# Where a Trainium2 network's tables begin: split weights 32 and 64 bytes from the split activations

## What is computed

```python
for i in range(2):                       # sparse attention, then an RWKV-7 mixer
    x = x + (dsa_mixer, rwkv7_mixer)[i](rms_norm(x, mixer_norm[i]), ...)
    x = x + sqrelu_mlp(rms_norm(x, mlp_norm[i]), w_up, w_down)   # relu(h @ w_up)**2 @ w_down
# then a short-convolution mixer and a dilated-attention mixer, each
h, gate = adaln_pre_norm(x, c, g, w_mod, b_mod)
x = x + gate * mixer(h, w_in, w_out)
return rms_norm(x)
```

## The kernel before

| table | remainder by 128 |
|---|---|
| `raw`, `w_hi`, `w_lo`, `X`, `const` (all slots) | 0 |
| `act_hi`, `act_lo`, set 0 and set 1 (all pieces) | 64 |
| `ff_hi`, `ff_lo` (both slots, all pieces) | 64 |
| `w_idx_hi`, `w_idx_lo`, piece kt (288 bytes each) | 64 + 32 kt |

## Time and profile before

### The profile page before, as it was taken

The page is one execution under the profiler, slowest core; times in us unless marked ns, Lnnn a source line. Parts: engine busy times, 40 slices in busy tenths (PEclk is TensorE's granted clock), DMA queues, the critical chain, the costliest instruction groups (busy, mean ns, idle before and its releaser), DMA issues.

```text
span 1066.7 us, 25458 instructions
## 1 busy us (share of the span) xinstructions
PE 1048.1 (98%) x10480; PEld 996.2 (93%) x10485; DVE 771.7 (72%) x1090; ACT 590.3 (55%) x900; POOL 120.4 (11%) x131
## 2 busy tenths in 40 slices
PE   9999999999999999999999999999999999999997
PEld 8966999999999899997899999999998999999985
DVE  5987666766789689768766676786676877775586
ACT  6586555555456783334555454564544667666452
POOL 0230010100000028841000000000000000000000
PEclk9999999999999999999999999999999999999999
DMA  8734687888634510002678777737653656556401
GB/s 308 251 90 137 216 286 266 271 296 280 204 122 155 163 61 5 3 11 74 217 250 287 255 252 264 276 121 228 197 192 112 212 181 199 171 195 196 143 2 59
DMA packets 83073, 192.23 MB, mean 180 GB/s; under 512 B 6000, under 2 KB 6912, under 8 KB 82992
## 3 DMA queue, kind: packets, MB, share of 16 engines
q1 hardware_dynamic: 74256, 159.93, 45.3%
q0 software_dynamic: 7584, 27.53, 7.8%
q10 hardware_dynamic: 1152, 3.59, 1.0%
HBM read 189.45 MB, written 1.05 MB: 179 GB/s over the span
## 4 chain that ended last, share of the span: by engine, by line
PE 88%; DVE 6%; issue 2%; ACT 2%; DMA 2%; POOL 0%; DVEq 0%; POOLq 0%; ACTq 0%
PE bank L2308 13%; PE bank L2310 13%; PE bank L2309 13%; PE bank L2659 5%; PE bank L2658 5%; PE bank L2660 5%; PE bank L2325 4%; PE bank L2345 4%; PE bank L2877 4%; PE bank L2275 2%; PE bank L2276 2%; PE bank L2277 2%; PE bank L2263 1%; PE bank L2265 1%; PE bank L2264 1%
## 5 line engine op out<-in xcount | busy, mean ns | idle before, releaser
L1350 DVE TENSOR_TENSOR w_lo<-raw,w_hi 128x1024 fp32r<-128x1024 f32 x295 | 357.8, 1223 | 199.2 <-ACT w_hi L737 198.7
L737 ACT ACTIVATE w_hi<-raw 128x1024 fp32r<-128x1024 f32 x295 | 310.3, 1059 | 291.4 <-PE bank L2310 150.4
L2308 PE MATMUL bank<-act_hi,w_hi 128*128 128x256 f32 x1200 | 334.0, 278 | 0.4 <-DVE w_lo L1350 0.3
L2309 PE MATMUL bank<-act_lo,w_hi 128*128 128x256 f32 x1200 | 332.9, 277 | 0.0
L2310 PE MATMUL bank<-act_hi,w_lo 128*128 128x256 f32 x1200 | 332.8, 277 | 0.0
L2308 PEld LDWEIGHTS bank<-act_hi,w_hi 128*128 128x128 f32 x1200 | 225.3, 188 | 1.7 <-DVE w_lo L1350 0.9
L2310 PEld LDWEIGHTS bank<-act_hi,w_lo 128*128 128x128 f32 x1200 | 225.3, 188 | 0.0
L2309 PEld LDWEIGHTS bank<-act_lo,w_hi 128*128 128x128 f32 x1200 | 225.0, 187 | 0.0
L2658 PE MATMUL bank<-w_hi,ff_hi 128*128 128x256 f32 x512 | 141.5, 276 | 0.0
L2659 PE MATMUL bank<-w_lo,ff_hi 128*128 128x256 f32 x512 | 141.5, 276 | 0.0
L2660 PE MATMUL bank<-w_hi,ff_lo 128*128 128x256 f32 x512 | 141.5, 276 | 0.0
(11 more groups left out here) (375 smaller groups left out, 1675.4 us busy)
## 6 DMA issues: line engine op xcount, KB each, us to landing
raw<-in_mlp_w_up_dram SPq DMA_DIRECT2D x64, 512.0 KB, 3.7
raw<-in_mlp_w_down_dram SPq DMA_DIRECT2D x64, 512.0 KB, 6.1
raw<-in_dil_w_in_dram SPq DMA_DIRECT2D x64, 512.0 KB, 4.1
mod_w<-in_w_mod_dram POOLq DMA_DIRECT2D x48, 512.0 KB, 5.9
raw<-in_conv_w_in_dram SPq DMA_DIRECT2D x32, 512.0 KB, 4.5
raw<-in_rwkv_w_rkv_dram SPq DMA_DIRECT2D x24, 512.0 KB, 4.1
raw<-in_dsa_w_in_dram SPq DMA_DIRECT2D x12, 512.0 KB, 8.1
raw<-in_dsa_w_o_dram SPq DMA_DIRECT2D x8, 512.0 KB, 4.5
```

The source lines that it names most:

```text
L737: act.activation(w_hi[:, slot, :], raw[:, slot, :], ACT.Copy).then_inc(hi_ready, 1)
L1350: dve.tensor_tensor(w_lo[:, slot, :], raw[:, slot, :], w_hi[:, slot, :].bitcast(F32), ALU.subtract).then_inc(lo_ready, 1)
L2308: pe.matmul(dst, w_hi[:, slot, at], hi[:, kt, :], start=begin, stop=False, skip_group_check=True)
L2309: pe.matmul(dst, w_hi[:, slot, at], lo[:, kt, :], start=False, stop=False, skip_group_check=True)
```

## The change

No instruction is added, taken away or moved on any engine. Seven small tables (`const_bf`, `pcol`, `mod_col`, `gain`, `stat`, `half_neg`, `less_k_a`) are declared ahead of `raw` instead of behind it. Their 4640 bytes are 36 times 128 and 32 over, so `raw`, `w_hi`, `w_lo`, `X` and `const` begin at remainder 32; the tables from `per_head` on stay where they were. `SET_OFF`, 8 elements or 32 bytes, is left between activation set 0 and set 1, and all behind it moves by 32. `FF_PAD`, 4 elements or 16 bytes, is left behind every piece of `ff_hi` and `ff_lo`.

```diff
+SET_OFF = 8
+FF_PAD = 4
...
+        n_const_bf = sum(int(np.prod(v.shape[1:])) for v in parts_bf.values()) - TILES * SEQ
+        const_bf = sb("const_bf", [P, n_const_bf], BF16)
+        pcol = sb("pcol", [P, PARAM_COLS])
+        mod_col = sb("mod_col", [P, 2, 2 * KT])
+        gain = sb("gain", [P, 2, KT])
+        stat = sb("stat", [P, 26])
+        half_neg = sb("half_neg", [P, 2])
+        less_k_a = sb("less_k_a", [P, KT])
         raw = sb("raw", [P, RING, GRAN])
...
-        n_const_bf = sum(int(np.prod(v.shape[1:])) for v in parts_bf.values()) - TILES * SEQ
         const = sb("const", [P, n_const])
-        const_bf = sb("const_bf", [P, n_const_bf], BF16)
         gate = sb("gate", [P, 2, D])
         scale_row = sb("scale_row", [P, D])
-        pcol = sb("pcol", [P, PARAM_COLS])
-        mod_col = sb("mod_col", [P, 2, 2 * KT])
-        gain = sb("gain", [P, 2, KT])
         c_col = sb("c_col", [P, KT])
-        stat = sb("stat", [P, 26])
-        half_neg = sb("half_neg", [P, 2])
-        less_k_a = sb("less_k_a", [P, KT])
         per_head = sb("per_head", [P, SEQ])
...
-            t("xn_under", [P, 3 * KT * SEQ])
+            t("xn_under", [P, 3 * KT * SEQ + SET_OFF])
...
-            t("act_hi0_lo0_under", [P, 2 * KT * SEQ])
+            t("act_hi0_lo0_under", [P, 2 * KT * SEQ + SET_OFF])
...
         for u in range(2):
+            if u == 1:
+                sb("set_off", [P, SET_OFF])
             act_hi.append(sb(f"act_hi{u}", [P, KT, SEQ], F32R))
             act_lo.append(sb(f"act_lo{u}", [P, KT, SEQ], F32R))
...
-                        hi=t("ff_hi", [P, 2, 4, SEQ], F32R), lo=t("ff_lo", [P, 2, 4, SEQ], F32R))
+                        hi=t("ff_hi", [P, 2, 4, SEQ + FF_PAD], F32R), lo=t("ff_lo", [P, 2, 4, SEQ + FF_PAD], F32R))
...
-                        act.activation(M["hi"][:, slot, 2 * b:2 * b + 2, :], M["sq"][:, b, :].rearrange("p (k t) -> p k t", k=2), ACT.Copy).then_inc(mid_hi, 1)
+                        act.activation(M["hi"][:, slot, 2 * b:2 * b + 2, 0:SEQ], M["sq"][:, b, :].rearrange("p (k t) -> p k t", k=2), ACT.Copy).then_inc(mid_hi, 1)
...
-                        at = (slice(None), slot, slice(2 * b, 2 * b + 2), slice(None))
+                        at = (slice(None), slot, slice(2 * b, 2 * b + 2), slice(0, SEQ))
```

## The result

| | before | changed |
|---|---|---|
| median of four runs | 1061.83 us | 1080.28 us |
| all four runs | 1061.2, 1061.2, 1062.45, 1068.3 | 1079.63, 1080.26, 1080.3, 1081.51 |
| span of the profiled execution | 1066.7 us | 1078.6 us |

The changed kernel is slower: ratio 1.0149, 95% interval 1.0106 to 1.0192; the two medians alone give 1.0174, inside it. Of all runs told of here one, a tenth run of all32 (1156.7 us, granted clock 0.848 where all others have 0.996 to 0.999), is left out of every count, median and ratio. Beside the times stands their spread. The changed kernel's runs lie within 2 us; before's lie in two groups, near 1061 and near 1068, and its profiled execution was the one of 1068.3 us (in every run listed the span is 1.6 to 1.8 us shorter than the time, and this span is 1066.7). Against a run of the lower group the change costs some 19 us, against the profiled one 12.

A forecast was written before the change was run, and what follows sets the result against it. TensorE's product count times spacing was taken as the bound. Three-part products gave -11 us, 512-column products, feed-forward down and other engines nothing: 1062.45 - 11 = 1051.5 us, range 1026 to 1073 (the forecast's own case 1048 to 1057).

The forecast's parts named there:

- The 512-column products: 384 products of 512 columns, at 233.3 ns each; no change taken, at most 6 us gain or 3.5 us loss.
- RWKV's second projection: Test stretch from 329.7 us on: its distance stays 64, so it may stay slow while its neighbours turn quick.
- The sign set for the slower rival: Feed-forwards holding more than 114 ns a product would show that the slower rival had come.
- slower rival: Feed-forwards fall to the slow cadence, 12 us, or 16 us with the convolution; about 1076 us; chance 0.15.
- the first term: Three-part products on activation set 0: distance 64 becomes 32, slow stretches take the quick cadence; 11 us gain.
- 270.6 us of slow stretches: Sum of eight slow stretches, 174.8 us of it dilated attention; 10.3 us gain if all took the quick cadence.
- Feed-forward, down: 1536 down products on padded pieces, nearly all quick already: nothing taken; distance zero in slot 1 costs 0.6 us at most.
- The index weights: Pieces at distances 0, 32, 64, 96: three products take 0.36 us at zero, 0.35 elsewhere, so zero costs some 3 ns each.
- Below the quick cadence: Rival: distance 64 burdens even the quick cadence, different distances remove it in part; 23 to 30 us, about 1035 us; chance 0.24.

The follow-up runs named there:

- all32: Changed kernel with activations and feed-forward pieces also moved 32 bytes and no padding, so the distance is 64 again; 1061.2 us, ratio 0.9984.
- set_dil: Kernel before plus four other-form products ahead of the dilated stretch's second projection and a single one eight products earlier; 1062.19 us.
- pad: Kernel before with only the 16 bytes of padding between feed-forward pieces added; 1079.73 us, ratio 1.0139.
- nopad: Changed kernel without the padding between feed-forward pieces (`FF_PAD = 0`); 1080.25 us, ratio 1.0138.
- dist48: Changed kernel without padding, both activation sets 16 bytes further on (distance 48, feed-forward pieces at 64); 1079.89 us, ratio 1.0138.
- toggle: Kernel before with four products of the other form (stationary activations) ahead of the dilated stretch's second projection; 1066.95 us, ratio 1.0049.
- w32: Changed kernel with only the weights' tables moved, activations and feed-forward pieces left in place, no padding (distance 32 everywhere); 1081.03 us, ratio 1.0145.
- dist16: Kernel before with both activation sets 16 bytes further on (distance 80, feed-forward pieces at 96); 1091.27 us, ratio 1.0243.
- form_all: Kernel before with one product of the other form at each of six places, among them feed-forwards and dilated stretch; 1069.11 us, ratio 1.0036.
- form_dil: Kernel before with one product of the other form ahead of the dilated stretch's second projection; 1068.53 us.
- set_dil_b: The same kernel as set_dil, run once more beside new runs of the kernel before; 1062.81 us.

## Why the prediction was wrong

**What held.** The kernel is bound by the number of products times their spacing; no wait, DMA or other engine had a part in the change, and the clock was the same. The 512-column products, taken at nothing, stayed: the last 36 take 8.40 us at distance 32, as before at 64. The two cadences of distance 64 are real, and a stretch keeps its own, depending on how it starts. RWKV's second projection stayed at 117.8, as said, but that was no test: at this same distance it is at 113.4 in all32 and in both profiles of set_dil. The sign set for the slower rival, feed-forwards over 114 ns a product, came: 157.0/1340.5 is 117.1.

**The step that failed** is the choice in the first term: "If every slow stretch took the quick cadence", and I took 11 us of gain "since the quick cadence is one that these very products are seen to run in". They were seen in it at distance 64 only. No row had a long stretch of them at another distance, and I let the two cadences of one distance stand for all. The runs put in its place: at 32 bytes 116.7 and 117.8 ns, so 764 quick products of the convolution lose 3.4 ns each (2.6 us), and the dilated stretch wins 1.1 ns each (1.3 us) instead of the 4.5 foretold. (The 270.6 us of slow stretches also held the 22.1 of RWKV's second projection, whose distance the change leaves alone: 0.8 us of the 11 had no ground.)

**Feed-forward, down, "I take nothing".** In seven of eight parts the changed pieces run at 114.4, 118.0, 118.5 and 117.6 ns, and in the last at some 118.8. Against 113.4 that is some 4 ns over 1536 products, 6 us. The up products lose 3.3 ns over some 1344, 4.4 us. Together that is a little over the 2 x 4.7 us measured, of which joints take a part back. The padding alone cost as much as the whole change: in pad the up products, still at distance 64, ran at 117.8 beside the padded pieces. In nopad the down products, at 64, ran at 117.8 beside up products at 32. Why dist48 holds 113.3 in its down products beside up products at 48 stays open. The prediction also counted 1536/8 = 192 products on the piece at distance zero; as slot 1 is used in the last step alone, there are 48.

**The index weights** did warn: three products took 0.35 us at 32, 64 and 96, that is 117 ns, and none 0.34. I read "32 is no better than 64" off them and gave it no part in the sum, where they also showed a group whose distance changes from piece to piece and that is slow throughout, at 64 too. Their 3 ns for "distance zero" were scatter: in the profile of toggle, with the same distances, the three products of piece 4 take 0.35 us.

**The rivals.** "Slower" named the right place (feed-forwards and convolution losing the quick cadence) and nearly the size, 12 to 16 us over the median, against 18.5. It had 0.15. Of its mechanism the loss at 32 bytes was right, though the cadence lost to was mostly a new one, 116.7, and not the slow one of before. The loss at 0 to 48 bytes in slot 1 is not refuted (118.8 ns there), but the padding cost as much in slot 0, at 80, 96 and 112, which the rival did not name. "Below the quick cadence" found no support: four distances gave no spacing under 113.3 ns. (Its estimate of some 38 us from 109.2 ns comes out at 35: 3611 products at 4.1 ns and 2297 at 8.6.)

**The size against the median.** The profile of before was an execution of the upper group. Its 174.8 slow microseconds counted as a loss that a layout might take away, while in most of the first runs, by their times, the dilated stretch was quick already: the gain of 11 us was some 6 us smaller from the start, and the loss to be had 6 us bigger. The spread of the three runs shown, 1061.2 to 1068.3, was the sign of it.

**Open.** What makes the start of the dilated stretch quick in one execution and slow in another; whether the distance counts by 128 or by 64; why it counts, and whether fetches of the two operands meet; and why one product of the other form leaves the slow cadence while four turn it over. Only groups of one and of four were run. No run here looks at an access.

## What to carry to other kernels

When a TensorE-bound kernel's products stand at two spacings at full clock, read the spacing by stretches before and after each gap and each change of form: here it was a kept state, not a cost of a line. Treat the distance between the starts of the moving and the stationary rounded-float32 operands as something to be measured, keep it alike in all tables, and do not pad pieces by 16 bytes unmeasured. Here 64 bytes by 128 was the best; equal starts were not tested. In this kernel every layout with another distance in it cost 18 to 30 us by its median over before's lower group. And when the runs of one kernel lie in two groups, find out to which the profile belongs before pricing anything from it.

## What the runs showed of the hardware

- Spacing of products with 128 stationary weight columns and 256 moving rounded-float32 columns, at granted clock 1.00, by distance of the two starts by 128 bytes: 32: 116.7 or 117.8 ns; 48: 118.3; 64: 113.3 or 117.8; 80: 120.0 or 118.3. With activations stationary and 256 weight columns moving: 32: 118.3 (w32); 48: 117.8 (dist48); 64: 113.3 or 117.8; 80: 118.8 (dist16's token part); 96: 117.3 or 118.7 (dist16's down products). With 512 weight columns moving: 233 at 64 and at 32.
- Moving weights and activations together by 32 bytes changes nothing clear of noise (all32: ratio 0.9984, 0.9951 to 1.0017). That the distance counts by 64 is not shown.
- At 64 a cadence is kept for over a thousand products, with VectorE, ScalarE and the DMA working beside (the DMA's share is 0.97 from 836 to 840 us of the profile of before, and 0.58 over the stretch). One product of the other form in between leaves 117.8 (quick ahead in form_all, slow ahead in form_dil); four turned 113.3 into 117.8 (toggle), and into 113.3 the 117.8 that a single one had left (set_dil, both profiles).
- Where the long dilated stretch is in one cadence or the other from execution to execution, a kernel's runs lie in two groups: of the 17 runs of before beside set_dil_b 9 lay under 1063 us and 8 over 1067. Their shares differ from one batch of runs to another (15 of 15 in the lower group beside set_dil, 8 of 23 beside form_dil).
- The Trainium skill, "SBUF — State Buffer", section "Who interferes with whom", gives the moving operand's read and the weight load's read a port each and says that TensorE never waits on anyone. The spread from 113.3 to 120.0 ns between 64 and 80 bytes of distance, at the same clock, does not agree with that rule: the two operands are not independent at this spacing. What they share no run shows.
